# Two transformer blocks on one core: the two-part weights of the token-form projections and of the cross output stand 32 bytes higher in their buffer slots

## The reference, cut to what matters

```python
proj = rmsnorm(h, norm_mix_g) @ w_in              # 1024 -> 2560: q, k, v, u, y
h = h + concat([attn, rec]) @ w_out               # 1024 -> 1024
h = h + memory_cross_attention(rmsnorm(h), rmsnorm(mem), w_cq, w_ck, w_cv, w_co)
h = h + square(relu(rmsnorm(h) @ w_mlp_in)) @ w_mlp_out
# and for each of two layers of the second block:
z = rmsnorm(x) @ w_in                             # the inputs of four mixers, and gates
x = x + merged @ w_out
x = x + (silu(g_part) * u_part) @ w_down          # g_part, u_part = rmsnorm(x) @ w_gate_up
```

## Time and profile before

| | |
|---|---|
| median of 3 runs | 1237.08 us (1236.97 to 1237.98) |
| span of the profiled execution, first to last instruction | 1235.1 us |
| the median less that span | 2.0 us |
| PE busy | 1227.5 us, 9196 matmuls |
| DVE busy, ACT busy | 852.4 us, 690.6 us |
| granted TensorE clock, mean | 1.000 (2.4 GHz) |

### The profile page before, as it was taken

The page is one execution under the profiler, slowest core; times in us unless marked ns, Lnnn a source line. Parts: engine busy times, 40 slices in busy tenths (PEclk is TensorE's granted clock), DMA queues, the critical chain, the costliest instruction groups (busy, mean ns, idle before and its releaser), DMA issues.

```text
span 1235.1 us, 22033 instructions
## 1 busy us (share of the span) xinstructions
PE 1227.5 (99%) x9196; PEld 1151.3 (93%) x9196; DVE 852.4 (69%) x1203; ACT 690.6 (56%) x1148; POOL 38.6 (3%) x88
## 2 busy tenths in 40 slices
PE   8999999999999999999999999999999999999998
PEld 8999989988899989999999998899899999999987
DVE  6997767654476778987766554658679986665543
ACT  5897665543367664872644443567555834544432
POOL 2100100000000000110100000000000100000000
PEclk9999999999999999999999999999999999999999
DMA  9642535555535333423555555444343425555552
GB/s 358 244 168 104 192 136 189 201 205 180 195 137 183 129 132 137 171 103 124 211 184 200 187 195 197 171 151 157 114 160 141 167 103 175 176 197 188 190 203 102
DMA packets 30611, 211.77 MB, mean 171 GB/s; under 512 B 3376, under 2 KB 3760, under 8 KB 5552
## 3 DMA queue, kind: packets, MB, share of 16 engines
q1 hardware_dynamic: 30224, 210.22, 47.8%
q10 hardware_dynamic: 288, 0.14, 0.0%
HBM read 209.29 MB, written 1.05 MB: 170 GB/s over the span
## 4 chain that ended last, share of the span: by engine, by line
PE 95%; ACT 2%; DVE 1%; issue 1%; DMA 1%; SPq 0%; DVEq 0%; ACTq 0%
PE bank L548 92%; PE bank L667 1%; PE bank L900 1%; ACT w_hi L1173 1%; DMA ring<-weight_pieces 1%; DVE x_lo L1803 0%; ACT W L1489 0%; ACT W L1173 0%; SPq L1060 0%; ACT W L1460 0%; ACT mem_hi L1173 0%; ACT W L1455 0%; DVE W L1648 0%; ACT L1489 0%; ACT L1465 0%
## 5 line engine op out<-in xcount | busy, mean ns | idle before, releaser
L1684 DVE TENSOR_TENSOR w_lo<-ring,w_hi 128x2048 fp32r<-128x2048 f32 (+1 forms) x180 | 409.0, 2272 | 239.1 <-ACT w_hi L1173 238.5
L1173 ACT ACTIVATE w_hi<-ring 128x1024 fp32r<-128x1024 f32 (+1 forms) x368 | 366.5, 1047 | 238.2 <-PE bank L548 221.6
L548 PE MATMUL bank<-x_hi,w_hi 128*128 128x256 f32 x1840 | 260.0, 280 | 2.1 <-issue 1.1
L548 PE MATMUL bank<-x_hi,w_lo 128*128 128x256 f32 x1840 | 252.4, 276 | 0.0
L548 PE MATMUL bank<-x_lo,w_hi 128*128 128x256 f32 x1840 | 247.3, 277 | 0.2
L548 PEld LDWEIGHTS bank<-x_hi,w_hi 128*128 128x128 f32 x1840 | 230.6, 188 | 5.5 <-ACT x_hi L1173 2.0
L548 PEld LDWEIGHTS bank<-x_hi,w_lo 128*128 128x128 f32 x1840 | 229.0, 188 | 0.3
L548 PEld LDWEIGHTS bank<-x_lo,w_hi 128*128 128x128 f32 x1840 | 226.6, 188 | 0.6 <-DVE x_lo L1803 0.6
L548 PE MATMUL bank<-W 128*128 128x128 f32 (+4 forms) x720 | 110.1, 326 | 1.5 <-DVE W L1709 1.2
L548 PEld LDWEIGHTS bank<-W 128*128 128x128 f32 (+3 forms) x720 | 87.7, 187 | 14.2 <-issue 5.1
L548 PE MATMUL bank<-w_hi,hid_hi 128*128 128x512 f32 x304 | 76.6, 389 | 0.0
(11 more groups left out here) (265 smaller groups left out, 1218.2 us busy)
## 6 DMA issues: line engine op xcount, KB each, us to landing
ring<-weight_pieces SPq DMA_DIRECT2D x191, 1024.0 KB, 4.8
const<-constants SPq DMA_DIRECT2D x1, 1376.5 KB, 12.2
W<-x_features SPq DMA_DIRECT2D x4, 256.0 KB, 5.4
ring<-weight_pieces SPq DMA_DIRECT2D x2, 512.0 KB, 6.2
h<-x SPq DMA_DIRECT2D x2, 512.0 KB, 6.3
W<-rg_weights SPq DMA_DIRECT2D x1, 1024.0 KB, 11.2
xs<-mem_features SPq DMA_DIRECT2D x1, 1024.0 KB, 12.6
oT<-mem SPq DMA_DIRECT2D x1, 1024.0 KB, 14.3
```

The costliest lines, as they stand in the source:

```text
L548: return nc.tensor.matmul(out, lhsT, rhs, start=first, stop=last)
L1173: return nc.scalar.activation(out, in_, ACT.Copy, scale=scale)
L1684: v.tensor_tensor(whole(w_lo, q), rows, whole(w_hi, q).bitcast(F32), ALU.subtract).then_inc(s_weight_low, 1)
```

## The change

The token-form pieces other than down and wd, that is v, cv, wout, b, c, hg and the cross output co, now start at word 8 of their slot (32 bytes up) in either slot. In slot 0 that is 32 bytes higher than before; in slot 1, where they started at word 32, it is word 8, so 96 bytes lower than before. In bytes divided by 256 their start goes from 96 in both slots to 128 in slot 0 and 0 in slot 1. Down and wd get the form name "row" and stay where they were. ACT's and DVE's writes of these pieces move with them. No instruction, wait, load or buffer is added or removed.

```diff
+ASIDE = 8
...
-            return [("proj", name, l, j, piece(n, "feat" if name in FEATURE else "tok")) for j in js]
+            return [("proj", name, l, j, piece(n, "feat" if name in FEATURE else "row" if name in ("down", "wd") else "tok")) for j in js]
+
+        def token_start(q):
+
+            _, n, form = split[q]
+            return (ASIDE if form == "tok" else BANK * (q % SPLITS)) * (n == PIECE)
...
-            c0 = half * (n // 2 + BANK) if form == "feat" else half * n // 2 + BANK * (q % SPLITS) * (n == PIECE)
+            c0 = half * (n // 2 + BANK) if form == "feat" else half * n // 2 + token_start(q)
...
-            c0 += BANK * (q % SPLITS) * (n == PIECE)
+            c0 += token_start(q)
...
-            c0 = (SLOT + BANK) * (q % SPLITS)
+            c0 = SLOT * (q % SPLITS) + token_start(q)
```

## The result

The changed kernel has a median of 1239.08 us (1238.22 to 1240.35, 21 runs) and the kernel before 1237.59 us (1236.20 to 1238.64, 21 runs): ratio 1.0014, 95% interval [1.0008, 1.0021], a loss of 1.0 to 2.6 us. The forecast was a gain of 4.1 us. The profiled executions differ by as much: the span went from 1235.1 to 1236.8 us.

The account below looks back on a forecast made before the run. PE was taken as the bound, busy 1227.5 of 1235.1 us. Gains of 3.6 + 0.5 + 0.3 less 0.3 given back made 4.1 us off the 1237.1 median: 1233.0 us, range 1231.0 to 1240.5.

Parts of the forecast that it names:

- part 1: 256-column token-form matmuls against x: 795 slow ones go from 117.8 to 113.3 ns, 3.6 us gained; v counted at nothing.
- The slower rival: Token-form matmuls: new place holds PE at 120 ns or above as reads collide at boundaries; 4.0 us lost, 1241.0; chance 0.20.
- point of decision: Mean distance of about 119 ns over the 1056 matmuls against x; below it the loss stays under 2.5 us.
- The rival of two rates and chance: Token-form matmuls: both rates stay, the moment PE resumes after a wait may decide; 1237.1 to 1238.3 us; chance 0.27.
- Parts 2 and 3: cv, 96 matmuls, to gain 0.5 us; co, 48 matmuls of 512 columns, to gain 0.3 us.
- Parts 4 and 5: ACT's and DVE's shifted writes cost nothing; slow starts after eight short PE waits give back 0.3 us.
- the forecast's own range: Whole kernel: 1231.8 us, with all gains of matmuls against x, cv, co and v, to 1234.6.

Follow-up runs that it names:

- the version at 112 bytes: Against the kernel before: token weights start 112 bytes above x in both slots, cross output 64 bytes above; 1234.54 us against 1236.93, ratio 0.9983.
- the map: Separate kernel computing nothing of the reference: bare matmul streams, moving operand's start stepped through 256 bytes against the stationary one's, after three waits; 113.3 ns at 112 bytes apart.
- the version at 64: Against the kernel before: token pieces and co exchange the two slots' old starts, so weights less x is 64 bytes, not 192; 1237.45 us, ratio 1.0006.

## Why the prediction was wrong

**The step that failed is part 1**, the term "the new place ends the slow rate": entered with -3.6 us, it measured +2.7 us over the 1152 matmuls, +2.4 without v. It priced the slow rate rightly: 795 x 4.5 ns = 3.6 us stands against 3.7 us of excess over 113.3 ns in the trace before, of which the version at 112 bytes takes 3.1. What failed was the choice of end. "Taking weights and x off a common grid looks more like the cure than the disease" rested on the earlier trace rows, where a step between the halves went with the fast rate, and stretched that to another quantity, the place by 64 bytes. The runs show a third thing: of 64 places one holds the fast rate after all three waits, two or three allow it, and the change went from one that allows it (192 bytes) to two that never did, 224 and 96. The map's stream gives these two 118.2 and 120.0 ns; the changed kernel has 118.31 and 119.82.

**The slower rival** had the sign, its mark in the trace (118 to 121 ns in all token pieces) and nearly the size in the worst case of part 1, 3.5 us, against 2.8 measured in excess distance over all 1152; but the loss in time is 1.5, because slot 0 stops at 118.3 instead of 120, because v's share is hidden, as the prediction had counted it, and because later waits of PE came out shorter, in part by chance. Its point of decision, 119 ns, is where the mean came out, 119.06, and it put the loss below that under 2.5 us. It is only by this rival that the measured time lies inside the stated range. Its mechanism (rows that cross boundaries together) is not shown: at 112 bytes the moving rows begin on no 64-byte boundary either, and that place is the best, while 116 bytes is among the worst.

**The rival of two rates and chance** is right for places that have two rates, 192 bytes in the kernel before and 64 in the version at 64: which one holds is settled anew at a wait, in the map as in the earlier trace rows, by something in that moment that no run here isolates. The earlier trace rows is a stronger case than the prediction made of it: the second piece begins at 385.95 us, so that the rate turns at the wait inside one piece. The rival was wrong that the new places would keep both rates.

**Parts 2 and 3.** cv was to gain 0.5 us and co 0.3: 11.52 to 11.53 us and 11.39 to 11.39. cv's rows only changed places in the list (its mem_lo matmuls from 119.5 to 118.0 and 116.6 ns, its mem_hi from 117.6 to 118.4 and 119.6). At 64 bytes co does give 0.2 us.

**Parts 4 and 5.** DVE's subtraction is at 2293 ns against 2292, so the copies cost nothing, as said. The give-back works in both directions: part of a loss is returned at a later wait (0.11 us at 408 us), as part of the gain was in the version at 112 bytes. One sum is off: parts 1 to 3 and v add up to 3.6 + 0.5 + 0.3 + 0.2 = 4.6 us, so that the forecast's own range ends at 1232.5 and not at 1231.8.

The rule of the Trainium skill that the prediction weighed ("TensorE: Matmul & The Clock Gate", Part 2, "Step-by-step: what each phase is for": the weight load has its own read port and takes nothing from the moving one) does not account for what these runs show: with nothing else running on the core, the same stream takes 113.3 to 123 ns a matmul by the distance of its two operands alone.

What stays open is why: whether the weight load's reads and the moving reads meet in SBUF, and why 112 bytes gives 113.3 ns and 108 gives 120. The runs show that the relative place decides which rates exist, not what collides.

## What to carry to other kernels

Where PE is the bound and one placement shows two distances between equal matmuls, measure the placements in a bare stream, every start after several waits, before moving anything: it takes one run, and here it gave the mean rates of the changed kernel within 0.2 ns and the one place that won. An argument from alignment gave the wrong sign. Take from the map only places that hold one rate after every wait, and try them in the kernel even then: the feat form at 192 bytes was fast in all four streams of the map and had two rates in the kernel, and a product that changes its place every few matmuls, as cv does, does not reach the rate of the stream.

## What the hardware did that I had not expected

- The distance between 256-column matmuls of this type (fp32r, one 128x128 weight load each) depends on the start of the moving operand less that of the stationary one, and a single word matters: 120.0, 113.3 and 123.2 ns at 108, 112 and 116 bytes. Whole multiples of 256 bytes do not: at 192 bytes in the kernel before, the four remainders by 1024 bytes have 116.5 to 116.9 ns.
- At 192 bytes (and 64) there are two steady rates, 113.3 and 117.8 ns. In the kernels run here, token form, they change only at a wait or at a piece with another place, and last until the next of these.
- The two forms differ: alternating 192 and 64 every four matmuls holds the feat form at 113.8 ns (90% fast), and the token form at 116.2 and 118.2.
- At 512 columns: 229.1 ns at 64 bytes, 233.3 at 192, 226.8 in down at 0 (228.3 in the map's single stream), so the good places there are others.
